# A fused two-layer encoder trunk: three changes of order, and in layer 1 the normalization's sums of squares on all partitions at once

## The reference

```python
def rms_norm(x, g):
    xf = x.astype(jnp.float32)
    y = xf * lax.rsqrt(jnp.mean(xf * xf, axis=-1, keepdims=True) + NORM_EPS)
    return (y * g.astype(jnp.float32)).astype(x.dtype)

def hybrid_layer(x, ...):
    h = rms_norm(x, norm_g)
    proj = jnp.einsum('bsd,de->bse', h, w_in) + b_in
    ...                       # A: indexer picks 128 keys a token, sparse attention
                              # B: chunked attention with a relative bias
                              # C: mLSTM matrix memory, chunkwise
    merged = jnp.sum(gate * y, axis=2)
    return x + jnp.einsum('bsd,de->bse', merged, w_out)
```

## Time and profile before

| | us |
|---|---|
| median of 3 runs (lowest to highest) | 1273.93 (1273.89 to 1274.03) |
| profiled execution, its own time | 1274.26 |
| its span (first to last instruction) | 1272.3 |
| TensorE busy in the span | 1261.3 |
| VectorE, ScalarE, GpSimd busy | 684.3, 632.7, 592.0 |

### The profile page before, as it was taken

The page is one execution under the profiler, slowest core; times in us unless marked ns, Lnnn a source line. Parts: engine busy times, 40 slices in busy tenths (PEclk is TensorE's granted clock), DMA queues, the critical chain, the costliest instruction groups (busy, mean ns, idle before and its releaser), DMA issues.

```text
span 1272.3 us, 19800 instructions
## 1 busy us (share of the span) xinstructions
PE 1261.3 (99%) x6494; PEld 1066.1 (84%) x6494; DVE 684.3 (54%) x1425; ACT 632.7 (50%) x1158; POOL 592.0 (47%) x758
## 2 busy tenths in 40 slices
PE   8999999999999999999999999999999999999998
PEld 7788888888888888888888888888888888888887
DVE  6898986865544211223677979767643621121144
ACT  6565667776434232333255465677854433323333
POOL 6654333332244554555674642343222455555463
PEclk9999999999999999999999999999999999999999
DMA  7223211221322323323242321122113223332331
GB/s 298 86 86 111 67 51 58 87 72 50 117 66 75 99 91 100 104 85 122 87 166 83 112 71 67 51 67 89 62 50 116 75 83 93 96 100 90 107 99 66
DMA packets 37047, 116.36 MB, mean 91 GB/s; under 512 B 4080, under 2 KB 4464, under 8 KB 36720
## 3 DMA queue, kind: packets, MB, share of 16 engines
q1 hardware_dynamic: 34672, 111.24, 26.6%
q10 hardware_dynamic: 2304, 4.20, 1.1%
HBM read 111.23 MB, written 4.19 MB: 91 GB/s over the span
## 4 chain that ended last, share of the span: by engine, by line
PE 94%; ACT 2%; DVE 1%; POOL 1%; DMA 1%; issue 1%; SPq 0%; DVEq 0%; ACTq 0%; POOLq 0%
PE acc L664 75%; PE ps_o L826 5%; PE ps_t L813 3%; PE ps_t L804 2%; PE ps_s L782 2%; PE ps_s L788 2%; PE ps_o L833 1%; DMA stage<-x_tok 1%; POOL w_lo L614 1%; PE acc L697 1%; PE spare L764 1%; PE ps_s L771 1%; PE spare L845 1%; ACT ak_s L1044 0%; POOL h_lo L626 0%
## 5 line engine op out<-in xcount | busy, mean ns | idle before, releaser
L614 POOL TENSOR_TENSOR w_lo<-w_raw,w_hi 128x256 fp32r<-128x256 f32 x744 | 579.4, 808 | 662.8 <-ACT w_hi L903 662.7
L664 PE MATMUL acc<-h_hi,w_hi 128*128 128x512 f32 x1112 | 445.2, 400 | 0.5 <-POOL h_lo L626 0.4
L664 PE MATMUL acc<-h_lo,w_hi 128*128 128x512 f32 x1112 | 435.4, 392 | 0.0
L664 PE MATMUL acc<-h_hi,w_lo 128*128 128x512 f32 x1112 | 290.4, 396 | 0.0
L903 ACT ACTIVATE w_hi<-w_raw 128x1024 fp32r<-128x1024 f32 (+1 forms) x210 | 201.8, 961 | 119.6 <-PE acc L664 90.9
L664 PEld LDWEIGHTS acc<-h_hi,w_hi 128*128 128x128 f32 x1112 | 209.2, 188 | 41.0 <-POOL h_lo L626 1.3
L664 PEld LDWEIGHTS acc<-h_lo,w_hi 128*128 128x128 f32 x1112 | 209.3, 188 | 39.1
L664 PEld LDWEIGHTS acc<-h_hi,w_lo 128*128 128x128 f32 x1112 | 204.3, 188 | 40.4
L1537 DVE SCALAR_TENSOR_TENSOR gated<-prob,acc 128x512 f32<-128x512 f32 x16 | 11.0, 688 | 246.7 <-PE acc L664 246.7
L1149 ACT ACTIVATE prob<-acc,par_half 128x512 f32<-128x512 f32 x48 | 33.0, 688 | 147.2 <-PE acc L664 147.2
L1120 ACT ACTIVATE prob_t<-ps_t 128x128 f32<-128x128 f32 (+3 forms) x128 | 54.5, 426 | 42.7 <-PE ps_t L813 42.5
(11 more groups left out here) (292 smaller groups left out, 1831.6 us busy)
## 6 DMA issues: line engine op xcount, KB each, us to landing
w_raw<-w_full SPq DMA_DIRECT2D x162, 512.0 KB, 3.5
w_raw<-w_mix SPq DMA_DIRECT2D x48, 256.0 KB, 2.6
rel<-rel ACTq DMA_DIRECT2D x16, 256.0 KB, 3.1
xT<-x SPq DMA_DIRECT2D x4, 512.0 KB, 6.5
stage<-x_tok SPq DMA_DIRECT2D x4, 512.0 KB, 9.9
xT<-x SPq DMA_DIRECT2D x1, 2048.0 KB, 9.2
x_kept<-xT SPq DMA_DIRECT2D x1, 2048.0 KB, 9.0
xT<-x_kept SPq DMA_DIRECT2D x1, 2048.0 KB, 8.1
```

Source lines behind the costliest of these rows:

```text
L614: last = pool.tensor_tensor(w_lo[:, slot, part, :], w_raw[:, raw, part, :], w_hi[:, slot, part, :].bitcast(F32), ALU.subtract)
L664: last = pe.matmul(acc[slot][:, :], w[:, slot, k, :], x[:, k, :], start=(place == 0), stop=(place == 3 * nk - 1))
```

## The change

In `schedule`, the `index` steps of query tile 2 stand behind the two `topk` rounds of their unit instead of ahead of them. In layer 0, GpSimd makes `h_lo` 1, 3 and 5 and only then the split of unit 4, and `h_lo` 7 is VectorE's. In the tail, the two products with `norm` are issued ahead of the wait for the newest squares, the two token tiles have a bank each, and the mean is made by two instructions. In layer 1, one matmul of 128x128 ones with `norm` puts the sums on all partitions; mean, root and reciprocal are made on 128x512 elements in SBUF (`norm`), and the diagonal and the second matmul are gone; L1288 and L1301 read the factor from `norm` instead of `spare`.

```diff
--- before.py
+++ after.py
@@ -163,14 +163,16 @@
             seq.append(("log", 0))
-        if u in INDEX_AT:
-            index(INDEX_AT[u])
+        if INDEX_AT.get(u) == NT - 1:
+            index(NT - 1)
         for step in STACKS_A.get(u - U_AK, ()):
...
                 seq.append(work.pop(0))
+        if INDEX_AT.get(u) == 2:
+            index(2)
     seq.append(("rel_bias", 0))
...
@@ -620,8 +622,10 @@
                 for c in range(1, DC, 2):
-                    if c == 5:
+                    if c == (7 if l == 0 else 5):
                         split(l, done - 1, done - 1, DC)
+                    if c == 7 and l == 0:
+                        break
                     pool.wait_ge(h_hi_ready, l * DC + c + 1)
...
@@ -674,11 +678,13 @@
                 pe.wait_ge(sq_ready, n)
-                for t in range(NT):
-                    last = pe.matmul(spare[:, t:t + 1], norm[:, t * P:(t + 1) * P], ones[:, 0:1], start=True, stop=True)
-                last.then_inc(spare_full, 1)
+                pe.matmul(spare[:, :], ones[:, 0:P], norm[:, :], start=True, stop=True).then_inc(spare_full, 1)
 
             def norm_spread(n):
+                if n > 0:
+                    pe.wait_ge(spare_free, n * SPARE_USES + 1 + FREE)
+                    pe.sem_inc(spare_full, 1)
+                    return
                 pe.wait_ge(spread_ready, n + 1)
...
@@ -700,12 +706,15 @@
 
-                for t in (2 * half, 2 * half + 1):
-                    sums = (spare, ps_o)[half][:, t:t + 1]
-                    pe.wait_ge(last_chain, 4 * half + 2)
-                    pe.matmul(sums, norm[:, t * P:(t + 1) * P], ones[:, 0:1], start=True, stop=False)
-                    pe.wait_ge(last_squares, half + 1)
-                    last = pe.matmul(sums, turn[:, t * P:(t + 1) * P], ones[:, 0:1], start=False, stop=True)
+                parts = [(spare, ps_o)[half][:, 0:1], (ps_o, spare)[half][:, 0:1]]
+                pe.wait_ge(last_chain, 4 * half + 2)
+                for p in range(2):
+                    t = 2 * half + p
+                    pe.matmul(parts[p], norm[:, t * P:(t + 1) * P], ones[:, 0:1], start=True, stop=False)
+                pe.wait_ge(last_squares, half + 1)
+                for p in range(2):
+                    t = 2 * half + p
+                    last = pe.matmul(parts[p], turn[:, t * P:(t + 1) * P], ones[:, 0:1], start=False, stop=True)
                 last.then_inc(last_sums, 1)
...
@@ -992,7 +1001,8 @@
                         act.wait_ge(mean_ready, l + 1)
-                        act.activation(tok[:, :], tok[:, :], ACT.Sqrt).then_inc(std_ready, 1)
+                        mean = tok if l == 0 else norm
+                        act.activation(mean[:, :], mean[:, :], ACT.Sqrt).then_inc(std_ready, 1)
                         act.wait_ge(params_in_s, l * 16 + 16)
...
@@ -1246,10 +1256,7 @@
                     dve.wait_ge(consts_in_s[0], 16)
-                else:
-                    dve.wait_ge(spare_full, n * SPARE_USES + 1)
-                dve.tensor_scalar(tok[:, :], spare[:, 0:NT] if n else row_sum[:, 0:NT], 1.0 / D, EPS, ALU.mult, ALU.add)\
-                   .then_inc(mean_ready, 1)
+                dve.tensor_scalar(tok[:, :], row_sum[:, 0:NT], 1.0 / D, EPS, ALU.mult, ALU.add).then_inc(mean_ready, 1)
 
...
@@ -1259,6 +1266,15 @@
 
+                if n > 0:
+                    dve.wait_ge(spare_full, n * SPARE_USES + 1)
+                    dve.tensor_scalar(norm[:, :], spare[:, :], 1.0 / D, EPS, ALU.mult, ALU.add).then_inc(mean_ready, 1)
+                    dve.sem_inc(spare_free, 1)
+                    dve.wait_ge(std_ready, n + 1)
+                    dve.reciprocal(norm[:, :], norm[:, :]).then_inc(tok_ready, 1)
+                    dve.wait_ge(tok_ready, n + 1)
+                    dve.wait_ge(spare_full, n * SPARE_USES + 2)
+                    return
                 norm_mean(n)
...
@@ -1285,10 +1301,14 @@
                             dve.wait_ge((h_even, h_odd)[n % 2], l * (DC // 2) + n // 2 - 1)
-                        dve.scalar_tensor_tensor(h_full[n % 4], xT[:, n, :], par[:, C_NORM + n:C_NORM + n + 1], spare[:, :],
+                        dve.scalar_tensor_tensor(h_full[n % 4], xT[:, n, :], par[:, C_NORM + n:C_NORM + n + 1], (spare, norm)[l][:, :],
                                                  ALU.mult, ALU.mult).then_inc(hf_ready, 1)
...
                             h_lo_part(n - 1)
+                        if n == DC - 1 and l == 0:
+                            dve.wait_ge(h_odd, DC // 2 - 1)
+                            dve.wait_ge(h_hi_ready, DC)
+                            dve.tensor_tensor(h_lo[:, n, :], h_full[n % 4], h_hi[:, n, :].bitcast(F32), ALU.subtract).then_inc(h_odd, 1)
                     elif kind == "turn_iw":
...
@@ -1298,7 +1318,7 @@
                             t = iq[:, n, :] if n < U_IK else ik[:, :] if n == U_IK else ak[:, :]
-                            link(dve.tensor_tensor(t, t, spare[:, :], ALU.mult))
+                            link(dve.tensor_tensor(t, t, (spare, norm)[l][:, :], ALU.mult))
                         dve.wait_ge(hf_ready, l * DC + DC)
...
@@ -1596,7 +1616,10 @@
                 dve.wait_ge(last_sums, half + 1)
-                dve.tensor_scalar(both, (spare, ps_o)[half][:, 2 * half:2 * half + 2], 1.0 / D, EPS, ALU.mult, ALU.add).then_inc(last_mean, 1)
+                for p in range(2):
+                    last = dve.tensor_scalar(tok[:, 2 * half + p:2 * half + p + 1], (spare, ps_o)[(half + p) % 2][:, 0:1], 1.0 / D, EPS,
+                                             ALU.mult, ALU.add)
+                last.then_inc(last_mean, 1)
                 dve.wait_ge(last_std, half + 1)
...
```

## The result

The changed kernel takes 1277.71 us (median of 9 runs, 1276.79 to 1278.34), the kernel before beside it 1274.03 (9 runs, 1273.89 to 1274.72). The ratio is 1.0027, with a 95% interval of 1.0019 to 1.0035: slower by 3.7 us, where 3.5 was forecast. The profiled execution took 1277.81, its span is 1275.7.

| stretch on TensorE | before | after | difference |
|---|---|---|---|
| start to unit 5 of layer 0 | 44.76 | 43.57 | -1.19 |
| from there to the sums of squares of layer 1 | 593.58 | 593.07 | -0.51 |
| from the sums to unit 4 of layer 1 | 20.59 | 26.27 | +5.68 |
| from there to unit 12, the index steps of layer 1 in it | 47.47 | 47.02 | -0.45 |
| from there to the end of the span | 565.90 | 565.77 | -0.13 |

What follows compares the result with a forecast made beforehand. TensorE, busy 1261.3 of 1272.3 us, bounds the kernel. Terms -0.95 - 0.7 - 0.05 + 4.4 + 0.8 = +3.5 on the profiled 1274.26 give 1277.8, as a median 1277.4; range 1271.9 to 1279.3.

Steps and rivals of the forecast that it cites:

- the lock: Layer 1: VectorE's two-SBUF-input instructions and GpSimd's slow each other; 0.44 us for each of twelve meetings, 5.3 in all.
- Layer 0, `h_lo`: Unit 4 of layer 0: the new `h_lo` order removes 0.95 of a 1.07 us wait; bounds 0.5 and 1.07.
- Index steps: Tile 2's third index step no longer waits for ScalarE's Relu: 0.35 us a layer, 0.7 for both; bounds 0 and 0.9.
- Tail: Product moved ahead of the wait, against a second mean instruction: net 0.05 us gained; bounds 0.2 gained, 0.15 lost.
- Reciprocal: Layer-1 factor: the reciprocal on 128x512 takes 3.35 us by the row's slope, so `h` 0 starts 1.2 later.
- Rivals one: Layer-1 factor: the reciprocal is quick, 0.7 us; the kernel then takes 1272.8 us; chance 0.13.
- three (4.4): Layer-1 factor: the reciprocal takes 4.4 us, with a longer stop; 1.3 more, 1278.7 us; chance 0.12.
- Rival four: Layer 1: at each meeting GpSimd waits for VectorE's whole instruction, 0.68 instead of 0.44 us; 1280.3 us; chance 0.03.
- rival two: Layer 1: VectorE and GpSimd hardly slow each other on `h`; 1272.8 us, or 1271.4 with a quick reciprocal; chance 0.15.
- Idle time of GpSimd: Layer 1: GpSimd, done with `h_lo` 1 at 649.6, waits for `h` 3, rounded by 650.8: 1.2 us idle.
- Pass 14: Unit 3 of layer 1: this pass, waiting for the last `h_lo`, starts 4.4 us later; bounds 0.6 and 5.5.
- The clock: Unit 3 of layer 1: TensorE's clock probably halves during its stop, costing 0.8 us; bounds 0 and 3.2.

Runs made afterwards that it cites:

- experiment three: The changed kernel, but the layer-1 reciprocal writes to the PSUM bank `spare`, and `h` and the scaling read it there: 1272.13 us, ratio 0.9985.
- experiment four: The changed kernel, but a cheap instruction writing a constant replaces the layer-1 reciprocal, the factor still in SBUF: 1276.07 us, ratio 1.0015.
- six: The changed kernel with the layer-1 factor in PSUM and layer 0's new `h_lo` order in layer 1 too: 1271.33 us, ratio 0.9978.
- experiment seven: The kernel before with only the order changes, the new `h_lo` order in both layers, layer-1 factor as before: 1272.18 us, ratio 0.9986.

## Why the prediction was right

The forecast, 1277.4 and slower, was right within 0.3 us, and its chain of reasons is the one that the traces show: a late `h`, the lock, a stop on GpSimd's `h_lo` in unit 3, the clock's fall in it. That it came so near is in part luck, since three terms missed by 0.3 to 0.8 each and the misses cancel. Term by term:

- **Layer 0, `h_lo`:** -0.95 taken, -1.06 measured (6.51 to 5.45), the upper bound. What I called just in time had time to spare: `h_lo` 5 was done at 32.3 for pass 10 at 34.96, `h_lo` 7 at 34.7 for pass 14 at 35.86, and half of the eight pieces of `w_lo`, those of unit 4, at about 35.6 for pass 16 at 36.32.
- **Index steps:** -0.7 taken. Unit 11 went from 706.40 - 699.05 = 7.35 us to 709.93 - 703.03 = 6.90 in layer 1, and from 81.34 - 74.00 = 7.34 to 79.67 - 72.76 = 6.91 in layer 0: -0.88, at the upper bound. I had counted the visible 0.32 and 0.03 for the restart in each layer; the restart makes some 0.12.
- **Tail:** -0.05 taken, -0.13 by the stretch from unit 12 to the end of the span, which holds more than the tail. Right within what they resolve.
- **Reciprocal:** 3.35 taken from the slope between 128x4 and 128x16, 3.353 measured. Rivals one (0.7) and three (4.4) are out. The chain through it gave 644.25 for `h` 0, though its terms add up to 644.15; measured is 642.48, and with the 1.70 that TensorE was earlier (638.34 - 636.64) that is 644.18.
- **The lock:** 0.44 for each of twelve meetings, 5.3 in all, taken; 4.67 measured. The twelve meetings were not the ones that I had counted: `h_lo` 2 fell into GpSimd's idle time and took 0.68, and the two scalings of `iq`, which also read `norm` now, met the last `h_lo`s. That makes thirteen, 0.36 for each; the other traces give 0.36 (factor in PSUM, four meetings), 0.39 (no reciprocal, twelve) and 0.44 (before, four). With 0.705 for a GpSimd piece and 0.68 for VectorE's instruction each meeting costs about half of one. Rival four (the whole instruction) is out, and rival two (hardly anything) too. The Trainium skill ("SBUF — State Buffer", Who interferes with whom) names the condition, two inputs in SBUF beside a GpSimd instruction that reads SBUF, and this agrees with both halves: 1.22 with `norm`, 0.73 with `spare`, same instruction. It also calls the pair of ports that the two engines share an exclusive lock. A wait for the whole of the other's instruction would be 0.68 a meeting, and by these rows the mean is 0.36 to 0.44.
- **Idle time of GpSimd:** 1.2 taken, 1.29 measured.
- **Pass 14:** +4.4 taken, for a last `h_lo` 17.3 after the split began. It was 16.8, and pass 14 came at 659.02 + 1.70 = 660.72 against 656.66: +4.06. The forecast's excess is the lock's.
- **The clock:** +0.8 taken, a guess within 0 to 3.2, +1.62 measured (2.27 to 3.89 from pass 14 to unit 4). This is the term that was mis-sized. The step that failed is "part of the slow time falls into the stop and into the second short wait": it does, but ten passes stand behind the second wait, in this trace nearly all of them had the slow clock, and at 0.20 a pass that is up to 2.0. It differs between executions: with the factor alone pass 14 to unit 4 took 663.61 - 660.58 = 3.03, so the clock cost 0.76 there. By the medians, filling the stop was worth 1.28.
- **Together** for layer 1: 4.06 + 1.62 = 5.68, where 5.2 was forecast; the orders -2.07 by the terms above, where -1.7 was forecast. The misses cancel for the most part.

What the prediction left open, and the experiments settle, is how the two causes stand to each other. Its sum reads as if the late `h` (1.2) and the lock (5.3) were alike. They are not. A late `h` without the lock costs unit 3 0.77 (experiment three). The lock without the late `h` costs 4.7 (experiment four, 1276.07, against six, 1271.33, where nothing waits for `h`; six also has the other order of `h_lo`, which by experiment seven brings nothing of its own). Both together cost 6.4. The last two include the clock. What stays open: why the slow clock lasts 6.8 us in the changed kernel's trace and half of that in two others (below).

## What to carry to other kernels

An operand that many VectorE instructions share may be better left in PSUM where GpSimd works beside them: a chain that computes in SBUF can write its last result to the bank (here the output of one instruction and the input of its two readers, 5.6 us). Price a lock on both engines, and on the one whose result the bound engine waits for; here GpSimd was hardly touched by the diff and set the time. And a stop of the matmul engine can cost more than its length, here 3.7 us and 1.6 behind it: look at the clock, and at how many passes lie behind the last wait.

## What the runs showed that I had not expected

- **The clock's timing.** The last pass before the stop ended at 653.43. By the stretch's mean (0.81 between 655 and 656) the clock fell at 655.6, 2.2 us later, and by the next one (0.78 between 662 and 663) it returned at 662.4, 5.3 after TensorE went on. With the reciprocal left out the clock fell at 655.8 and came back at 659.2, 3.2 after the end of a stop of 2.54. With the factor alone it fell only at 658.7, as TensorE went on after a stop of 3.71, and came back at 662.1. So the slow time was 6.8 us in the first and 3.4 in the other two, and the price of about the same stop was 1.62 in one trace and 0.76 in another. The stretches of the kernel without the reciprocal, and of the one with the factor alone:

```profile
655.00:656.00 1.00, 0.00 (x1) 0.01 (x1) 1.00 (x1) 0.99 (x1) 1.00 (x2) 0.90 0.54 164
...
659.00:660.00 1.00, 1.00 (x5) 0.77 (x5) 0.82 (x2) 0.00 (x0) 1.00 (x2) 0.90 0.00 0
```
```profile
658.00:659.00 1.00, 0.29 (x1) 0.30 (x2) 1.00 (x1) 0.77 (x1) 1.00 (x2) 0.86 0.81 262
...
662.00:663.00 1.00, 1.00 (x6) 0.82 (x5) 0.78 (x3) 0.00 (x0) 1.00 (x2) 0.93 0.00 0
```

- **The reciprocal's pace** is even over the whole range: 177 ns for 4 elements a partition, 252 for 16, 3353 for 512, which is 6.25 ns for each further one, beside about 1.3 for other instructions (0.68 us for 512). Writing to PSUM instead of SBUF changes nothing (3.36). The Trainium skill ("VectorE: DVE Perf Modes", First, the fixed hardware budget) has a repeat count of 8 for the divide; an estimate from that page, 8 cycles of its 0.96 GHz an element, would be 8.3 ns, and the measured pace is 6 such cycles.
- **Work that saves time.** Sixteen products whose results nobody uses took 1.3 us off by the medians, and in the profiled execution the clock stayed up.
